# Stick-breaking attention heads: sums of later key blocks made by VectorE before the suffix products

## Chip, cores and metric
One core of one Trainium2 chip. The metric is device time in microseconds of one launch; lower is better.

## What is computed
A long fp32 program of two transformer-like blocks on 512 tokens of 1024 features. The part that matters here is the stick-breaking attention of the second block, 8 heads of 64 features:

```python
z = einsum('bqhd,bshd->bhqs', q, k) * scale
past = key_pos[None, :] < qpos[:, None]
log_keep = where(past, log_sigmoid(-z), 0.0)
suffix = cumsum(log_keep, axis=3, reverse=True) - log_keep   # sum over the later keys
w = where(past, exp(log_sigmoid(z) + suffix), 0.0)
out = einsum('bhqs,bshd->bqhd', w, v)
```

Beside it, on VectorE, the same stretch of time holds the top-k selection for the DSA attention that follows: for three blocks of 128 queries the 128 largest of 256, 384 and 512 scores, as a mask.

## The kernel before
Keys lie on the 128 partitions and queries along the free dimension. A head's scores are four key blocks `kt` = 0 to 3, of 512, 384, 256 and 128 queries (query blocks before the key block are causally empty). They stand behind one another at columns `ZOFF` = 0, 512, 1024, 896, + of a region of 1280 columns in PSUM; two regions take turns over the heads. Block 3 lies at 896 and block 2 at 1024, so each of them begins and ends inside a bank.

Each head h passes these steps:
- TensorE, `sb_scores(h)`: three fp32r products per key block (high and low halves) and the causal mask. From h = 2 on they wait for the exponential of head h - 2, whose region they overwrite, and for the low halves of their query and key jobs (`job_lo`).
- ScalarE, `sb_softplus(h)`: Abs, Exp and Ln over 1280 columns into `zw`.
- VectorE, `sb_max(h)` (L2578): max(z, 0) + zw into `spt`, which is the softplus, in fp32. It waits for the values of head h - 2, which read the same buffer of `spt`.
- TensorE, `sb_suffix(h)` (L1128): for each key block kt the sum of softplus over later keys is subtracted from z in PSUM: a product with `negtri` (-1 on the diagonal and on one side of it) for the block's own keys, and one with `negone` (all -1) for every later block k2. These are plain fp32 products, two recorded passes each. Loop: kt over 0 to 3, k2 over kt to 3.
- ScalarE: the exponential of the region into `spt` (L1784), the weights.
- TensorE, `sb_values(h)` (L1139): 10 products of 64 columns. VectorE, `sb_out(h)`: the copy of the head to `T0`.

Engines run their own lists in order, tied by semaphores. TensorE's list per head: `sb_suffix(h)`, transposes of a query job (`sb_job`, in heads 1 and 3; `dsa_job` in head 5), `sb_values(h - 1)`, `sb_scores(h + 2)`, transposes of a key job, which wait for the low half of the job before. VectorE's list per head (L2598 to L2620): `sb_max(h + 1)`, the low half of a job (heads 1, 3, 5), `sb_out(h - 1)`, column sums of loaded weights (`sum_step`), top-k steps (`topk`, max8 and match-replace, L2407 and L2409) as dealt out by `TOPK_SB`, in heads 1, 3 and 5 a second low half between them. After the last head all three masks `Mk` must be written (L2422) before TensorE goes on with `dsa_scores(1)` (L1205).

Of the kernel before, what the change touches and what calls it, by code (L numbers as in the profile page):

```python
# [6 lines left out]
ALU = mybir.AluOpType  # L7
# [7 lines left out]
P = 128  # L15
SEQ, CTX, D = 512, 256, 1024
# [50 lines left out]
ZOFF = (0, 512, 1024, 896)  # L67
# [82 lines left out]
def program(nc, t, out):  # L150
    ctx = ExitStack()
    with ctx:
# [3 lines left out]
        def sem(name):  # L156
            return ctx.enter_context(nc.semaphore(name))
# [47 lines left out]
        def s2(name, shape, dt=F32):  # L205
            return e2.enter_context(nc.sbuf_tensor(name, shape, dt))
# [12 lines left out]
        negtri = s2("negtri", [P, P])  # L219
        negone = s2("negone", [P, P])  # L220
# [5 lines left out]
                                                                     ("ixH", "ixL", "izH", "izL")])[1:]  # L226
        zw = s2("zw", [P, 2, 1280])
        spt = s2("spt", [P, 2, 1280])
        e2.close()


# [7 lines left out]
        def s3(name, shape, dt=F32):  # L239
# [80 lines left out]
        rp_rd, odd_rp, zero_rd, ixT, ix_hi, ix_lo, ixs_rd, ixr_rd, ix_acc, msk_rd = [sem(n) for n in (  # L320
            "rp_rd", "odd_rp", "zero_rd", "ixT", "ix_hi", "ix_lo", "ixs_rd", "ixr_rd", "ix_acc", "msk_rd")]
        jobT, job_hi, job_lo = sem("jobT"), sem("job_hi"), sem("job_lo")
        z_rd, zmin_rd, zexp_rd, zln_rd, sp_rd, arg_rd, wgt_rd, sv_rd, so_rd = [sem(n) for n in (
            "z_rd", "zmin_rd", "zexp_rd", "zln_rd", "sp_rd", "arg_rd", "wgt_rd", "sv_rd", "so_rd")]
        ds_rd, dmx_rd, dp_rd, dt_rd, dpv_rd, do_rd = [sem(n) for n in ("ds_rd", "dmx_rd", "dp_rd", "dt_rd", "dpv_rd", "do_rd")]
# [396 lines left out]
        def _(pe):  # L722
            mm, tr = nc.tensor.matmul, nc.tensor.transpose
# [7 lines left out]
            for j in range(4):  # L731
                last = tr(X[:, 0, VCW + TAPS * j:VCW + TAPS * j + TAPS], cwr[0:TAPS, j * P:j * P + P],
                          ident[0:TAPS, 0:TAPS])
# [241 lines left out]
            for j in range(4):  # L975
                last = mm(acc[:, 0, :], onesD[:], cy[:, j], start=(j == 0), stop=(j == 3))
# [3 lines left out]
            for j in range(4):  # L980
                for tt in range(TT):
                    last = tr(oTp[j][:, tt * P:tt * P + P], qtok[:, tt, j * P:j * P + P], ident[:])
                last.then_inc(oT, 1)
            for j in range(4):
                pe.wait_ge(csq_rd, j + 1)
                last = mm(acc[:, 3, :], onesD[:], sgt[:, j % 2], start=(j == 0), stop=(j == 3))
# [121 lines left out]
            def region(h):  # L1108
                return ps[:, 4 - 4 * (h % 2):7 - 4 * (h % 2), :].rearrange("p b n -> p (b n)")
# [18 lines left out]
            def sb_suffix(h):  # L1128
                z, s_ = region(h), spt[:, h % 2]
                pe.wait_ge(sp_rd, h + 1)  # L1130
                for kt in range(4):
                    for k2 in range(kt, 4):
                        w = SEQ - k2 * P
                        o0 = ZOFF[kt] + (k2 - kt) * P
                        last = mm(z[:, o0:o0 + w], negtri[:] if k2 == kt else negone[:], s_[:, ZOFF[k2]:ZOFF[k2] + w],
                                  start=False, stop=True, skip_group_check=True)
                last.then_inc(arg_rd, 1)

            def sb_values(h):  # L1139
# [36 lines left out]
            for h in range(NH):  # L1176
                sb_suffix(h)
                if h in (1, 3):
                    sb_job(h + 3)
                if h == 5:  # L1180
                    dsa_job(8)
                if h >= 1:
                    sb_values(h - 1)
                if h + 2 < NH:
                    sb_scores(h + 2)
                if h in SB_TURN:
                    pe.wait_ge(job_lo, h + 4)
                    turn_group(SB_TURN[h])
                if h in (1, 3):
                    sb_job(h + 4)  # L1190
                if h == 5:
                    dsa_job(9)
# [848 lines left out]
        def _(dve):  # L2041
            V = nc.vector
# [200 lines left out]
            q = tapped  # L2243
# [331 lines left out]
            def region(h):  # L2575
                return ps[:, 4 - 4 * (h % 2):7 - 4 * (h % 2), :].rearrange("p b n -> p (b n)")[:, 0:1280]

            def sb_max(h):  # L2578
                dve.wait_ge(zln_rd, h + 1)
                if h >= 2:  # L2580
                    dve.wait_ge(sv_rd, h - 1)
                V.scalar_tensor_tensor(spt[:, h % 2], region(h), 0.0, zw[:, h % 2], ALU.max, ALU.add).then_inc(sp_rd, 1)

            def sb_out(h):
                dve.wait_ge(sv_rd, h + 1)
                V.tensor_copy(T0[:, :, h * HD:h * HD + HD], ps[:, 3, 0:256].rearrange("p (t d) -> p t d", t=4))\
                    .then_inc(so_rd, 1)
# [3 lines left out]
            even_tile_out(4, 1)  # L2591
            topks(4, 1)
            sb_max(0)
            even_tile_out(4, 3)
            sb_low(2)
            sb_low(3)
            split_low(NC1 + 11)
            for h in range(NH):  # L2598
                steps = range(TOPK_SB[h], TOPK_SB[h + 1])
                if h + 1 < NH:  # L2600
                    sb_max(h + 1)
                if h in (1, 3):
                    sb_low(h + 3)
                if h == 5:
                    job_low(8, 0, 7, True)
                if h >= 1:
                    sb_out(h - 1)
                for kt in range(4):
                    if h < 4 and kt % 2 == 0:
                        sum_step(13, 2 * h + kt // 2)  # L2610
                    if kt == 1 and h in SB_TURN:
                        group_columns(SB_TURN[h])
                    if kt < len(steps) - 1:
                        topk(steps[kt])
                if h in (1, 3):
                    sb_low(h + 4)
                if h == 5:
                    job_low(9, 0, 7, False)
                if h < 7:
                    topk(steps[-1])  # L2620
# [428 lines left out]
```

## Time and profile before

| | us |
|---|---|
| median of 3 runs | 1762.8 |
| lowest, highest | 1760.67, 1763.5 |
| the profiled execution | 1767.19 |
| its span | 1765.5 |
| stage of the 8 heads (suffix of head 0 to the copy of head 7) | 489 to 577 |

The profile is one execution. Its page gives shares of the whole span; the order of time gives instructions of an engine with start, duration and, in brackets, the idle time before one and what ended it.

### The profile page before, as it was taken

How to read it: one execution, taken by the hardware profiler on the slowest of the kernel's cores; microseconds unless marked ns; L12 is line 12 of the kernel's file. 1: busy time of each engine (PE TensorE's matmuls, PEld its weight loads, DVE VectorE, ACT ScalarE, POOL GpSimd, SP SyncE). 2: the span in 40 equal slices, each digit the busy share in tenths (PEclk: the TensorE clock that was granted, in tenths of full speed). 3: DMA queues.
4: the chain of work that ended last, by engine and by line, in shares of the span. 5: the costliest groups of instructions: out<-in, count | busy, mean ns of one | idle time of the engine just before them, and what ended most of it. 6: DMA issues, size and time to landing. Idle time of an engine off the chain costs nothing.

```text
span 1765.5 us, 22789 instructions
## 1 busy us (share of the span) xinstructions
PE 1662.8 (94%) x8951; PEld 1370.4 (78%) x8957; DVE 1009.1 (57%) x1435; ACT 658.6 (37%) x887; POOL 322.9 (18%) x250
## 2 busy tenths in 40 slices
PE   4999999999898998999999999899979899999999
PEld 3897787888776886788887887777757688888887
DVE  3568898777878658533333345757576733333243
ACT  4323465432354424423332223434463533333121
POOL 0000000000000003788885011224301100000011
PEclk8999999999999999999999999999989999999999
DMA  7645300352210323565564323221102133332321
GB/s 270 216 144 190 97 1 1 116 177 85 95 52 21 96 93 100 165 184 179 184 189 161 113 86 95 73 72 48 49 25 72 51 116 95 95 95 89 130 88 48
DMA packets 145605, 187.93 MB, mean 106 GB/s; under 512 B 7053, under 2 KB 104565, under 8 KB 145524
## 3 DMA queue, kind: packets, MB, share of 16 engines
q1 hardware_dynamic: 145524, 186.82, 32.9%
q8 instruction: 55, 0.90, 0.2%
q14 instruction: 26, 0.21, 0.0%
HBM read 184.70 MB, written 2.10 MB: 106 GB/s over the span
## 4 chain that ended last, share of the span: by engine, by line
PE 64%; DVE 13%; POOL 9%; issue 6%; DMA 4%; ACT 3%; SPq 1%; another core or an unknown queue 0%; POOLq 0%; DVEq 0%; ACTq 0%
PE ps L841 7%; PE ps L843 7%; PE ps L842 7%; POOL mraw L628 4%; POOL msum L635 4%; DMA mraw<-in_w_mod_dram 3%; PE ps L1349 2%; PE ps L1351 2%; PE ps L1350 2%; PE ps L1346 2%; PE ps L1342 2%; PE ps L1343 2%; PE ps L1405 2%; PE ps L1407 2%; PE ps L1406 2%
## 5 line engine op out<-in xcount | busy, mean ns | idle before, releaser
L1537 ACT ACTIVATE whi<-wraw 128x2048 fp32r<-128x2048 f32 x71 | 135.8, 1913 | 305.0 <-PE ps L843 210.2
L2052 DVE TENSOR_TENSOR wlo<-wraw,whi 128x2048 fp32r<-128x2048 f32 x64 | 148.2, 2316 | 152.9 <-ACT whi L1537 152.7
L2808 DVE TENSOR_TENSOR wlo<-wraw,whi 128x2048 fp32r<-128x2048 f32 x22 | 51.5, 2341 | 203.4 <-ACT whi L1901 203.4
L1342 PE MATMUL ps<-uH,whi 128*128 128x512 f32 x352 | 141.2, 401 | 9.8 <-ACT uH L1869 8.3
L1343 PE MATMUL ps<-uH,wlo 128*128 128x512 f32 x352 | 139.7, 397 | 0.0
L841 PE MATMUL ps<-hH,whi 128*128 128x512 f32 x352 | 139.1, 395 | 0.0
L843 PE MATMUL ps<-hH,wlo 128*128 128x512 f32 x352 | 137.8, 391 | 0.0
L842 PE MATMUL ps<-hL,whi 128*128 128x512 f32 x352 | 137.7, 391 | 0.0
L1350 PE MATMUL ps<-uL,whi 128*128 128x512 f32 x352 | 136.9, 389 | 0.0
L1349 PE MATMUL ps<-uH,whi 128*128 128x512 f32 x352 | 136.9, 389 | 0.0
L1351 PE MATMUL ps<-uH,wlo 128*128 128x512 f32 x352 | 136.9, 389 | 0.0
L1346 PE MATMUL ps<-uL,whi 128*128 128x512 f32 x352 | 111.5, 399 | 4.2 <-DVE uL L2747 4.2
L635 POOL TENSOR_TENSOR msum<-msum,mraw 128x512 f32<-128x512 f32 x66 | 107.6, 1631 | 5.2
L841 PE MATMUL ps<-uH,whi 128*128 128x512 f32 x256 | 103.0, 402 | 0.0
L843 PE MATMUL ps<-uH,wlo 128*128 128x512 f32 x256 | 100.3, 392 | 0.0
L842 PE MATMUL ps<-uL,whi 128*128 128x512 f32 x256 | 100.2, 391 | 0.0
L628 POOL TENSOR_TENSOR mraw<-mraw,cpad 128x1024 f32<-128x1024 f32 x44 | 84.3, 1916 | 55.9 <-PE ps L756 43.1
L1905 ACT ACTIVATE whi<-wraw 128x2048 fp32r<-128x2048 f32 x22 | 42.2, 1919 | 137.3 <-PE ps L1351 137.3
L1898 ACT ACT_TABLE_LOAD x22 | 28.2, 1283 | 173.4 <-PE ps L1346 173.4
L2119 DVE SCALAR_TENSOR_TENSOR cy<-utp,cols,cy 128x512 f32<-128x512 f32 x116 | 87.0, 750 | 3.4
L1342 PEld LDWEIGHTS ps<-uH,whi 128*128 128x128 f32 x352 | 67.8, 193 | 26.2 <-issue 12.2
L1346 PEld LDWEIGHTS ps<-uL,whi 128*128 128x128 f32 x352 | 67.6, 193 | 19.7 <-DVE uL L2747 5.4
(500 smaller groups left out, 3839.7 us busy)
## 6 DMA issues: line engine op xcount, KB each, us to landing
mraw<-in_w_mod_dram SPq DMA_DIRECT2D x104, 512.0 KB, 3.8
wraw<-in_w_gate_dram SPq DMA_DIRECT2D x22, 1024.0 KB, 5.3
wraw<-in_w_up_dram SPq DMA_DIRECT2D x22, 1024.0 KB, 5.4
wraw<-in_w_down_dram SPq DMA_DIRECT2D x16, 1024.0 KB, 5.2
wraw<-in_w_in_dram SPq DMA_DIRECT2D x11, 1024.0 KB, 5.5
mfirst<-in_w_mod_dram SPq DMA_DIRECT2D x16, 512.0 KB, 7.6
wraw<-in_w_in_even_dram SPq DMA_DIRECT2D x8, 1024.0 KB, 6.3
wraw<-in_w_in_odd_dram SPq DMA_DIRECT2D x16, 512.0 KB, 4.5
```

Of the source, the lines that this page charges most:

```text
L628: g.tensor_tensor(w, w, cpad[:, 2 * kp:2 * kp + 2, 2:3].to_broadcast([P, 2, GW]), ALU.mult).then_inc(msum_rd, 1)
L635: g.tensor_tensor(msum[:], msum[:], w[:, kk], ALU.add).then_inc(msum_rd, 1)
L841: mm(o, h, xh[:, k0 + k], start=(first and k == 0), stop=False)
L842: mm(o, h, xl[:, k0 + k], start=False, stop=False)
L843: last = mm(o, l, xh[:, k0 + k], start=False, stop=(done and k == nk - 1))
L1342: mm(o[m], w_[0][m][:, k], uH[:, k], start=(k == 0), stop=False)
L1343: mm(o[m], w_[1][m][:, k], uH[:, k], start=False, stop=False)
L1346: last = mm(o[m], w_[0][m][:, k], uL[:, k], start=False, stop=(k == KT - 1))
L1349: mm(o[m], w_[0][m][:, k], uH[:, k], start=(k == 0), stop=False)
L1350: mm(o[m], w_[0][m][:, k], uL[:, k], start=False, stop=False)
L1351: last = mm(o[m], w_[1][m][:, k], uH[:, k], start=False, stop=(k == KT - 1))
L2052: V.tensor_tensor(wlo[:, n % 2, :], wraw[:, n % 2, :], whi[:, n % 2, :].bitcast(F32), ALU.subtract).then_inc(lo_done, 1)
```

## The change
For each head VectorE forms three sums of softplus blocks in a new buffer `later` (two heads, three blocks of 128 columns). In the kernel's layout they are: for queries of block 2, keys of blocks 1 + 2; for queries of block 3, blocks 2 + 3; and for queries of block 3, blocks 1 + 2 + 3. One `tensor_tensor` of 256 elements makes the first and second at once, one of 128 elements adds block 1 to the latter. Each is waited for by a semaphore of its own, `add_rd`.

TensorE first does the four triangular products of 512, 384, 256 and 128 columns, then three products of 128 columns with `negone` for the nearest later block, read straight from `spt`. Then it waits for the sums and does two products, of 128 and 256 columns. With `negone` this is 768 columns a head in five products, where it was 1280 in six. Nothing else moves.

```diff
+        later = s2("later", [P, 2, 3, P])
@@ sb_suffix(h), TensorE
                 for kt in range(4):
-                    for k2 in range(kt, 4):
-                        w = SEQ - k2 * P
-                        o0 = ZOFF[kt] + (k2 - kt) * P
-                        last = mm(z[:, o0:o0 + w], negtri[:] if k2 == kt else negone[:], s_[:, ZOFF[k2]:ZOFF[k2] + w],
-                                  start=False, stop=True, skip_group_check=True)
+                    r = slice(ZOFF[kt], ZOFF[kt] + SEQ - kt * P)
+                    mm(z[:, r], negtri[:], s_[:, r], start=False, stop=False, skip_group_check=True)
+
+                def later_keys(kt, q, blocks, x):
+                    o0 = ZOFF[kt] + (q - kt) * P
+                    return mm(z[:, o0:o0 + blocks * P], negone[:], x, start=False, stop=True, skip_group_check=True)
+
+                later_keys(2, 3, 1, s_[:, ZOFF[3]:ZOFF[3] + P])
+                later_keys(1, 2, 1, s_[:, ZOFF[2]:ZOFF[2] + P])
+                later_keys(0, 1, 1, s_[:, ZOFF[1]:ZOFF[1] + P])
+                pe.wait_ge(add_rd, 2 * h + 2)
+                later_keys(1, 3, 1, later[:, h % 2, 2])
+                last = later_keys(0, 2, 2, later[:, h % 2, 0:2, :].rearrange("p b n -> p (b n)"))
                 last.then_inc(arg_rd, 1)
@@ sb_max(h), VectorE
                 V.scalar_tensor_tensor(spt[:, h % 2], region(h), 0.0, zw[:, h % 2], ALU.max, ALU.add).then_inc(sp_rd, 1)
+                dve.wait_ge(sp_rd, h + 1)
+                if h >= 2:
+                    dve.wait_ge(arg_rd, h - 1)
+                s_, sums = spt[:, h % 2], later[:, h % 2]
+                others = s_[:, ZOFF[1] + P:ZOFF[1] + 5 * P].rearrange("p (i n) -> p i n", n=2 * P)[:, :, 0:P]
+                V.tensor_tensor(sums[:, 0:3:2], s_[:, ZOFF[2]:ZOFF[2] + 2 * P].rearrange("p (i n) -> p i n", n=P), others,
+                                ALU.add).then_inc(add_rd, 1)
+                dve.wait_ge(add_rd, 2 * h + 1)
+                V.tensor_tensor(sums[:, 1], sums[:, 2], s_[:, ZOFF[1] + 2 * P:ZOFF[1] + 3 * P], ALU.add).then_inc(add_rd, 1)
```

## Rows read from the trace of the kernel before

**Rows 1.** The page: span, then engine, busy us, share, instructions
```profile
span 1765.5 us, 22789 instructions
...
PE 1662.8 (94%) x8951; PEld 1370.4 (78%) x8957; DVE 1009.1 (57%) x1435; ACT 658.6 (37%) x887; POOL 322.9 (18%) x250
```

**Rows 2.** The chain that ended last, 538 to 600: start us, us, what
```profile
549.23 1.49 DVE spt L2582
...
570.66 0.44 DVE Mk L2422
...
571.14 0.58 PE ps L1205
```

**Rows 3.** TensorE in order of time: start, us, line, operands, [idle before <-releaser]
```profile
497.35 0.47 PE L1122 MATMUL ps<-uH 128*128 128x512 f32 x1 [3.52 <-ACT spt L1784]
...
511.30 1.02 PE L1135 MATMUL ps<-spt,negtri 128*128 128x512 f32 x2
...
512.16 1.46 PE L1135 MATMUL ps<-spt,negone 128*128 128x384 f32 x6
...
515.64 2.34 PE L1146 MATMUL ps<-T,spt 128*128 128x64 f32 x20
...
531.10 0.66 PE L1105 MATMUL ps<-ident,T 128*128 128x128 f32 x4 [1.23 <-DVE uL L2569]
...
538.60 0.50 PE L1122 MATMUL ps<-uH 128*128 128x512 f32 x1 [0.34 <-DVE uL L2566]
...
560.93 1.12 PE L1135 MATMUL ps<-spt,negtri 128*128 128x512 f32 x2 [1.68 <-DVE spt L2582]
...
571.14 0.58 PE L1205 MATMUL ps<-uH 128*128 128x256 f32 x1 [3.02 <-DVE Mk L2422]
```

**Rows 4.** VectorE in order of time, the same columns
```profile
508.66 1.49 DVE L2582 SCALAR_TENSOR_TENSOR spt<-ps,zw 128x1280 f32<-128x1280 f32 x1 [4.19 <-PE ps L1146]
...
511.00 0.74 DVE L2323 SCALAR_TENSOR_TENSOR msum<-mraw,cpad,msum 128x512 f32<-128x512 f32 x1
...
511.66 0.55 DVE L2407 MAX8 m<-work 128x8 f32<-128x384 f32 x1
...
518.73 1.49 DVE L2582 SCALAR_TENSOR_TENSOR spt<-ps,zw 128x1280 f32<-128x1280 f32 x1
...
528.95 1.49 DVE L2582 SCALAR_TENSOR_TENSOR spt<-ps,zw 128x1280 f32<-128x1280 f32 x1
...
540.10 1.49 DVE L2582 SCALAR_TENSOR_TENSOR spt<-ps,zw 128x1280 f32<-128x1280 f32 x1
...
549.23 1.49 DVE L2582 SCALAR_TENSOR_TENSOR spt<-ps,zw 128x1280 f32<-128x1280 f32 x1 [2.82 <-PE ps L1146]
...
559.38 1.49 DVE L2582 SCALAR_TENSOR_TENSOR spt<-ps,zw 128x1280 f32<-128x1280 f32 x1 [0.24 <-PE ps L1146]
...
569.15 0.75 DVE L2420 SCALAR_TENSOR_TENSOR ptd<-ptd,cnt 128x512 f32<-128x512 f32 x1
...
569.93 0.69 DVE L2421 TENSOR_TENSOR work<-work,ptd 128x512 f32<-128x512 f32 x1
```

**Rows 5.** VectorE by shape: line, operation, shape, count | busy us, mean ns
```profile
L2481 DVE TENSOR_TENSOR tmp<-T,ropet 128x256 f32<-128x256 f32 x4 | 1.7, 417 | 0.0
...
L2160 DVE TENSOR_TENSOR tmp<-kvt,ropet 128x128 f32<-128x128 f32 x2 | 0.6, 284 | 0.0
...
L2894 DVE TENSOR_TENSOR tmp<-T,ropet 128x256 f32<-128x256 f32 x6 | 4.7, 775 | 0.0
```

**Rows 6.** Stretches of 2 us: busy by engine (count), then PEclk, DMA share, GB/s
```profile
498.00:500.00 2.00, 2.00 (x12) 1.54 (x11) 1.97 (x3) 0.00 (x0) 0.00 (x0) 0.67 0.00 0
...
502.00:504.00 2.00, 2.00 (x9) 1.28 (x8) 1.93 (x6) 1.94 (x3) 0.00 (x0) 0.98 0.00 0
...
570.00:572.00 2.00, 0.86 (x4) 0.77 (x5) 1.58 (x4) 0.35 (x2) 0.00 (x0) 0.59 0.00 0
...
580.00:582.00 2.00, 1.86 (x16) 1.62 (x15) 1.10 (x2) 0.80 (x4) 0.00 (x0) 0.85 0.00 0
```

More of the change, by code:

```diff
@@ L322, in program @@
         jobT, job_hi, job_lo = sem("jobT"), sem("job_hi"), sem("job_lo")
+        add_rd = sem("add_rd")
         z_rd, zmin_rd, zexp_rd, zln_rd, sp_rd, arg_rd, wgt_rd, sv_rd, so_rd = [sem(n) for n in (
```

## Prediction

> **What bounds the kernel now.** I read the page first [rows 1]: TensorE is busy for 94% of the span, VectorE for 57%. That average would make a cut of TensorE work look like a gain and added VectorE work look free. So I looked only at the stage that is changed, from 485 to 577 us. The chain that ended last [rows 2] passes from TensorE to `sb_max(6)` at 549.23 and closes the stage on VectorE: the mask `Mk` of the top-k selection is written at 570.66, and only then does TensorE go on at 571.14 with the DSA scores, after 3.02 us without work.
>
> TensorE's order of time [rows 3] shows one head: suffix products at 511.30, and the values of the head before at 515.64. After that it waits for VectorE four times in the stage: 1.23 us at 531.10 (for the low halves of job 6), 0.34 us at 538.60 (for those of job 7), 1.68 us at 560.93 (for `sb_max(7)`) and 3.02 us at 571.14. VectorE's order of time [rows 4] is the other side: it waits 4.19 us at 508.66, then runs from `sb_max(2)` without a wait through `sb_max(3)` (518.73), `sb_max(4)` (528.95) and `sb_max(5)` (540.10), waits 2.82 us at 549.23 and 0.24 us at 559.38, both for the values on TensorE, and is not idle again before the mask. Between its 8 maxima it works through the top-k steps that `TOPK_SB` dealt out. So the two engines are nearly even, VectorE ends the stage, and TensorE has time left.
>
> **TensorE's saving.** The products of a head with the full matrix go from 1280 columns to 768, those with the triangle stay at 1280. The 512 columns saved are as many as the first triangular product has: its two passes start at 511.30 and the next product at 512.16 [rows 3], so 0.86 us a head, off a suffix of 4.34 us (511.30 to 515.64); 3.48 us are left. For eight heads that is 6.9 us of TensorE work.
>
> **VectorE's addition.** Two adds a head. The 256-element add takes 0.417 us in the mean of four in the rotation of the DSA queries and the 128-element one 0.284 us [rows 5]; one of the same 256-element shape takes 0.775 us in a later stage where GpSimd works too. GpSimd has nothing to do in this stage after 489 us, so I take the lower one and keep the other as an end. The adds wait for results of VectorE itself. A waited instruction starts 0.03 us after its predecessor's end (569.15 + 0.75 to 569.93), an unwaited one 0.08 us before it (511.00 + 0.74 to 511.66) [rows 4]. So a head pays 0.11 us because the first add must see `sb_max` finished, 0.42 + 0.03 us for the first add, 0.28 - 0.08 us for the second: A = 0.77 us, 6.1 us for eight heads. Ends: 0.54 us (the two durations less an overlap of 0.08 each, as if no wait cost anything) and 1.13 us (the slow row in place of 0.42).
> The Trainium skill ("VectorE: DVE Perf Modes", The DRAIN you can't avoid) says of a semaphore between two operations that it "costs nothing extra here". The two spacings above do not agree: 0.11 us. By that rule A would be at its lower end and the sum below 1.15 us smaller; the rows decide.
>
> **New waits.** TensorE waits for the second add only after four triangular products and three single blocks, 1280 + 384 columns, 0.86 x 1664/512 = 2.8 us after it could start; the adds are ready 0.75 us after the maximum. This wait is free. Its cover would be gone only if the adds took over 2.8 us. VectorE's new wait for the suffix of two heads before (`arg_rd`) is met before the maximum can start, as that waits for later work. Behind the adds on VectorE stand the low halves, the copy of the finished head, the column sums (with them the issue of the next weight loads on the SyncE queue) and the top-k steps: all are 0.77 us late for each add before them. That is the real price.
>
> **The sum, head by head**, as shifts against the old times (+ is later):
> - Heads 0 and 1 before `sb_max(2)`: the first saving is lost, since scores(2) wait at 497.35 for ScalarE's exponential [rows 3], which was behind its own work. The adds of heads 0 and 1 go into VectorE's 4.19 us of idle time. Suffix(1) ends 0.86 earlier, so `sb_max(2)` starts at -0.86.
> - `sb_max(3)`: VectorE ran without a wait, -0.86 + 0.77 = -0.09. `sb_max(4)`: +0.68. Low half of job 7 (L2566, which ends the wait at 538.60 [rows 3]): behind the adds of head 4, +1.45. `sb_max(5)` the same.
> - TensorE: scores(6) wait for that low half, so +1.45; suffix(5) gives back 0.86; values(4), for which `sb_max(6)` waits, are at +0.59. VectorE alone would be at 1.45 + 0.77 - 2.82 = -0.60, so TensorE sets it: `sb_max(6)` at +0.59. VectorE's big idle of 2.82 us shrinks to 1.2 and does not vanish.
> - `sb_max(7)`: 0.59 + 0.77 - 0.24 = +1.12. The mask: 1.12 + 0.77 = +1.89.
> In one line: 5A - 2 x 0.86 - 0.24 = +1.89 us. Five adds lie on the path, two savings do, the other six savings lie beside waits. TensorE's last gap grows to about 5.3 us.
> After 571 us nothing in the chain is tied to a fixed time. Later waits (TensorE waits once for GpSimd's sums near 957 us) shift as a whole, so I pass the delay on fully. With A = 0.54 the sum is +0.74, with A = 1.13 +3.7.
>
> **The clock.** The granted clock [rows 6] is 0.67 from 498 to 500 and 0.98 from 502 to 504: TensorE ran at the lower level (1.2 GHz) from about 498.7 to 502.1, after the 3.52 us wait. Likewise from about 570.4 (0.59 of full over 570 to 572) to 580.6 (0.85 over 580 to 582), around the 3.02 us wait; that stretch ended in sparse work. The waits of 1.23 and 1.68 us brought no fall. In the new kernel the wait before job 7's transposes grows from 1.23 us: scores(5) end 0.9 earlier, the low half of job 6 comes 0.68 + 0.77 later, 3.6 us in all. If the clock falls there for a stretch like the first (3.4 us), TensorE loses 1.7 us; 1.2 us of that lies under its wait for job 7's low half (0.34 us before; the low half is 1.45 us later and suffix(4) with values(3) only 0.59: 1.2 us), leaving 0.5 us. I add these 0.5 us: +2.4 us. The longer waits at 493 and 568 may move the other two stretches by a microsecond or two: +-0.9 us, no sign taken.
>
> The profiled execution took 1767.2 us (span 1765.5), 0.25% over the median 1762.8 of the runs; the sum is made against the profile and +2.4 us carried to the median: **1765.2 us**.
>
> **Rivals.**
> 1. *The clock falls and stays* (slower). Place: suffix(4) and values(3), after the new 3.6 us gap. Point: from 2.4 us at the lower level on, all that is lost (half of each microsecond) is no longer covered. With a stretch as long as the second one (10.2 us) TensorE loses 5.1, 1.2 of it covered: +3.9 on top of 1.9, 1768.6 us. For it: both waits over 3 us are tied to the lower level. Against: the suffix is dense work, and after 497.35 dense work had the higher level back in 4.7 us. The Trainium skill ("TensorE: Matmul & The Clock Gate", HAM oscillation — how this bites in real kernels) describes just this, a gap for input after which TensorE restarts at half rate, and speaks against any change that widens such gaps. Beside it, the slow 256-element add (A = 1.13) gives +3.7 + 0.5, 1767.0 us. Together 25%.
> 2. *The adds are as good as hidden* (no change). A at its lower end, and the stretch at 571 us no longer than its work: 1762 to 1763.5 us. For it: VectorE idles 7.3 us in the stage. Against: 4.2 of these lie before the part that matters. 14%.
> 3. *TensorE is the bound* (faster). Where the page's 94% held for this stage too, eight savings would count, less what ScalarE covers in head 0: 7 x 0.86 = 6.0, 1756.8 us. Against: TensorE's four waits for VectorE. A partial form, where VectorE catches up through its wait at 549.23, still needs the adds at under half their rows to pass -3.5 us. 6%.
> The forecast itself, +0.8 to +3.5 us, has 55%.
>
> **How the numbers follow.** 0.2% is 3.5 us, about what a measurement here can tell from no change (the three runs span 2.8 us). Faster by more: 0.06. Within: the forecast, rival 2 and the weaker part of rival 1: 0.70. Slower by more: 0.24. Range: below, rival 2 with a run's spread, 1761.5; above, the long low-clock stretch, 1769.0.
>
> **What would show it.** Right: a suffix of 3.5 us a head with no wait inside; adds of 0.42 and 0.28 us right behind each maximum; VectorE without a wait from `sb_max(2)` to the end of head 4; an idle of 1 to 2 us before `sb_max(6)`; a 3 to 4 us wait of TensorE before job 7's transposes; `Mk` near 572.5 and TensorE idle for 5 us before it. Wrong: a wait at the second group of products, an add of 0.7 us, a mask earlier than 570, or a later stage that absorbs the shift or doubles it.

## The result and the profile after

| | before | after |
|---|---|---|
| median, us | 1762.8 | 1767.58 |
| lowest, highest of 13 runs each | 1758.8, 1764.67 | 1763.99, 1774.97 |
| ratio, 95% interval | | 1.0034 (1.0021 to 1.0046) |
| the profiled execution (its span) | 1767.19 (1765.5) | 1770.69 (1769.0) |

The change costs time: by the ratio 6.0 us of 1762.8, between 3.7 and 8.1, by the medians 4.8. The two profiled executions lie 3.5 us apart. Forecast were +2.4 us, in a range up to 1769.0, and, at 70%, "not to be told from no change"; the slower side, by more than 3.5 us, had 24%, and the interval of the ratio lies on that side. All ratios are of fast executions alone: they leave out one of topk_behind_filled, of 9255.55 us, and two of the kernel before, of 2368.17 and 3299.25 us.

The page of after, span and engines:

```profile
span 1769.0 us, 22785 instructions
...
PE 1658.8 (94%) x8941; PEld 1366.5 (77%) x8941; DVE 1014.6 (57%) x1451; ACT 658.7 (37%) x887; POOL 323.7 (18%) x250
```

TensorE works 4.0 us less than in [rows 1] and VectorE 5.5 us more, and the shares are the same 94% and 57%. The page gives no hint of why the kernel is slower.

TensorE in order of time, the same columns as in [rows 3]; suffix(2) begins at 511.23:

```profile
496.44 0.77 PE L1124 MATMUL ps<-uH 128*128 128x512 f32 x1 [4.37 <-ACT spt L1794]
...
500.85 2.88 PE L1135 MATMUL ps<-spt,negtri 128*128 128x512 f32 x8
...
511.23 2.32 PE L1135 MATMUL ps<-spt,negtri 128*128 128x512 f32 x8
513.39 0.83 PE L1139 MATMUL ps<-spt,negone 128*128 128x128 f32 x6
514.06 0.82 PE L1139 MATMUL ps<-later,negone 128*128 128x128 f32 x4
514.72 2.34 PE L1156 MATMUL ps<-T,spt 128*128 128x64 f32 x20
```

Four triangular products in a row (x8: two passes each), three with `negone` on softplus blocks, two on the sums. From 511.23 to 514.72 it takes 3.49 us, where it took 4.34, and between its groups no wait is shown. Its waits later in the stage:

```profile
532.60 1.12 PE L1107 MATMUL ps<-ident,T 128*128 128x128 f32 x4 [3.66 <-DVE uL L2579]
...
562.39 3.78 PE L1135 MATMUL ps<-spt,negtri 128*128 128x512 f32 x8 [2.32 <-DVE spt L2592]
...
573.39 0.48 PE L1215 MATMUL ps<-uH 128*128 128x256 f32 x1 [2.99 <-DVE Mk L2432]
...
574.33 4.37 PE L1156 MATMUL ps<-T,spt 128*128 128x64 f32 x20
```

The wait before job 7's transposes has grown from 1.23 to 3.66 us, the one before suffix(7) from 1.68 to 2.32; before the DSA scores it is 2.99 us, as it was (3.02), only 2.25 us later, and not the 5 us I had expected, as the suffix of head 7 ran at the lower clock (below) and took 5.25 us (562.39 to 567.64) in place of 3.49. The last line is the values of head 7, which ran at the lower clock before the change too:

```profile
572.18 4.37 PE L1146 MATMUL ps<-T,spt 128*128 128x64 f32 x20
```

VectorE in order of time:

```profile
497.39 1.49 DVE L2592 SCALAR_TENSOR_TENSOR spt<-ps,zw 128x1280 f32<-128x1280 f32 x1
...
507.81 1.49 DVE L2592 SCALAR_TENSOR_TENSOR spt<-ps,zw 128x1280 f32<-128x1280 f32 x1 [3.46 <-PE ps L1156]
509.33 0.42 DVE L2598 TENSOR_TENSOR later<-spt 128x256 f32<-128x256 f32 x1
509.79 0.29 DVE L2601 TENSOR_TENSOR later<-later,spt 128x128 f32<-128x128 f32 x1
...
518.67 1.49 DVE L2592 SCALAR_TENSOR_TENSOR spt<-ps,zw 128x1280 f32<-128x1280 f32 x1
...
529.67 1.49 DVE L2592 SCALAR_TENSOR_TENSOR spt<-ps,zw 128x1280 f32<-128x1280 f32 x1
...
541.60 1.49 DVE L2592 SCALAR_TENSOR_TENSOR spt<-ps,zw 128x1280 f32<-128x1280 f32 x1
```

```profile
550.12 1.49 DVE L2592 SCALAR_TENSOR_TENSOR spt<-ps,zw 128x1280 f32<-128x1280 f32 x1 [1.42 <-PE ps L1156]
...
560.85 1.49 DVE L2592 SCALAR_TENSOR_TENSOR spt<-ps,zw 128x1280 f32<-128x1280 f32 x1
...
572.91 0.43 DVE L2432 TENSOR_SCALAR Mk<-work 128x512 bf16<-128x512 f32 x1
```

Each maximum is followed by its two adds, 0.42 and 0.29 us. There is no wait shown from 507.81 to the end of head 4; before `sb_max(6)` it is 1.42 us where it was 2.82 in [rows 4]. The clock of TensorE in stretches of 2 us, columns as in [rows 6]:

```profile
494.00:496.00 2.00, 0.00 (x0) 0.00 (x0) 1.46 (x2) 1.98 (x2) 0.00 (x0) 0.76 0.00 0
496.00:498.00 2.00, 1.55 (x5) 0.97 (x5) 1.97 (x2) 0.30 (x1) 0.00 (x0) 0.50 0.00 0
...
500.00:502.00 2.00, 2.00 (x8) 1.48 (x8) 1.90 (x7) 0.91 (x1) 0.00 (x0) 0.54 0.02 4
...
532.00:534.00 2.00, 1.40 (x5) 1.25 (x6) 2.00 (x4) 1.01 (x2) 0.00 (x0) 0.64 0.00 0
534.00:536.00 2.00, 2.00 (x4) 0.81 (x3) 1.90 (x6) 1.00 (x2) 0.00 (x0) 0.50 0.00 0
...
564.00:566.00 2.00, 2.00 (x7) 1.48 (x6) 1.90 (x6) 0.00 (x0) 0.00 (x0) 0.50 0.00 0
```

I measure the stage from the start of `sb_max(1)` to the start of the last mask `Mk`, both on VectorE. Before: 498.30 to 570.66, 72.36 us. After: 497.39 to 572.91, 75.52 us, so **+3.16 us**. Two lines of the kernel before on which this and a later reading rest are `sb_max(1)` on VectorE and the start of suffix(1) on TensorE:

```profile
498.30 1.49 DVE L2582 SCALAR_TENSOR_TENSOR spt<-ps,zw 128x1280 f32<-128x1280 f32 x1
```

```profile
500.64 1.79 PE L1135 MATMUL ps<-spt,negtri 128*128 128x512 f32 x2
```

The stretch ahead of the stage was 0.91 us shorter in this execution, though nothing is changed there, and the one behind it 1.3 us longer (1769.0 - 572.91 = 1196.1 against 1194.8).

How long TensorE was at the lower clock in the whole execution can be added up from windows of 4 us: about 99 us in both profiled executions. The changed one had 10 us more of it between 480 and 588 (25 against 15), and 7 us less from there to the end (51 against 58). So more time at the lower clock does not explain the 1.3 us behind the stage; they stay open.

### The profile page after: what moved, and what is told of

The parts are those of the page before. It is cut to its first block, busy times and chain, and to the rows that moved or that the text cites. A ratio compares the mean times of both kernels' runs of the same rounds, so it can differ in the third digit from the quotient of the medians.

```text
span 1769.0 us, 22785 instructions
## 1 busy us (share of the span) xinstructions
PE 1658.8 (94%) x8941; PEld 1366.5 (77%) x8941; DVE 1014.6 (57%) x1451; ACT 658.7 (37%) x887; POOL 323.7 (18%) x250
## 4 chain that ended last, share of the span: by engine, by line
PE 63%; DVE 14%; POOL 9%; issue 6%; DMA 4%; ACT 4%; SPq 1%; POOLq 0%; DVEq 0%; ACTq 0%
PE ps L843 7%; PE ps L844 7%; PE ps L845 7%; POOL mraw L630 4%; POOL msum L637 4%; DMA mraw<-in_w_mod_dram 2%; PE ps L1352 2%; PE ps L1360 2%; PE ps L1353 2%; PE ps L1356 2%; PE ps L1359 2%; PE ps L1361 2%; PE ps L1415 2%; PE ps L1417 2%; PE ps L1416 2%
```

## Experiments

All were timed in 5 rounds against the kernel before on the same chip. "Stage" is the interval defined above, from each kernel's profiled execution; "to `dsa_scores(1)`" is from the same start to the DSA scores on TensorE that need the last mask; "rest" is from the last mask to the end of the span.

| kernel | ratio (95%) | stage, us | to `dsa_scores(1)`, us | rest, us |
|---|---|---|---|---|
| before | 1 | 72.36 | 72.84 | 1194.8 |
| after | 1.0034 (1.0021 to 1.0046) | 75.52 | 76.00 | 1196.1 |
| triangles_first | 0.9995 (0.9984 to 1.0005) | 72.30 | 72.78 | 1191.2 |
| adds_alone | 1.0039 (1.0024 to 1.0053) | 79.49 | 79.97 | 1195.1 |
| saving_alone | 0.9997 (0.9986 to 1.0009) | 71.14 | 71.62 | 1196.3 |
| adds_twice | 1.0043 (1.0029 to 1.0057) | 78.69 | 79.17 | 1194.4 |
| adds_behind | 1.0011 (0.9998 to 1.0024) | 74.57 | 75.05 | 1192.9 |
| before_filled | 0.9969 (0.9956 to 0.9982) | 70.91 | 72.12 | 1190.0 |
| after_filled | 0.9991 (0.9977 to 1.0005) | 77.85 | 78.33 | 1190.0 |
| before_topk_early | 0.9966 (0.9951 to 0.9982) | 67.50 | 69.48 | 1191.8 |
| after_topk_early | 0.9950 (0.9931 to 0.9968) | 66.99 | 68.61 | 1190.7 |
| before_topk_filled | 0.9948 (0.9933 to 0.9964) | 66.10 | 69.41 | 1191.6 |
| topk_adds_behind | 0.9953 (0.9937 to 0.9968) | 65.03 | 65.51 | 1191.6 |
| topk_behind_filled | 0.9961 (0.9943 to 0.9978) | 64.49 | 64.97 | 1191.7 |

The theory (VECTOR): VectorE ends the stage; five pairs of adds lie on its path to the mask and two savings of TensorE count. The rival (CLOCK): the adds are as good as hidden, and the loss comes from wider waits of TensorE and the lower clock behind them.

**The order alone** (triangles_first).

```diff
 for kt in range(4):
-    for k2 in range(kt, 4): ... negtri if k2 == kt else negone ...
+    negtri product of the block
+for kt in range(3):
+    for k2 in range(kt + 1, 4): ... negone ...   # all 1280 columns
```

> The order alone: all four triangular products, then the six with the full matrix, 1280 columns each, no sums. All theories: no change, within 0.5 us; each suffix 4.34 us as before. If alternating the stationary matrices cost TensorE anything, it would be faster by that, up to 8 x 0.2 = 1.6 us.

Ratio 0.9995, stage 72.30 for 72.36 us. The order is neutral, and no gain from fewer changes of the stationary matrix can be seen.

**The adds alone** (adds_alone): the changed VectorE, the old products on TensorE. Before its last block TensorE waits for the sums, which are ready long before.

```diff
 for kt in range(4):
+    if kt == 3:
+        pe.wait_ge(add_rd, 2 * h + 2)
     for k2 in range(kt, 4): ... as before, 1280 columns with negone ...
```

> VectorE makes the sums as in the changed kernel, TensorE keeps its 1280 columns with the full matrix and does not read the sums. Theory VECTOR (VectorE's adds of heads 2 to 7 lie on the path to the masks, 0.77 us each, the first in idle time): the mask 5 x 0.77 = 3.9 us later against the stage's start, total +3.9 to +5 us. Theory CLOCK (the adds are as good as hidden, the loss comes from wider waits of TensorE and the lower clock after them): the waits widen less than in the changed kernel as nothing ends earlier on TensorE, total 0 to +1 us.

Ratio 1.0039, which is 6.9 us (4.2 to 9.3; VECTOR expected 3.9 to 5, CLOCK 0 to 1), and the stage is 7.1 us longer, 3.3 us more than VECTOR's 3.85. Neither theory alone gives that. Two starts of `sb_max` on VectorE (heads 4 and 5), then the clock at 532 and at 538:

```profile
530.12 1.49 DVE L2586 SCALAR_TENSOR_TENSOR spt<-ps,zw 128x1280 f32<-128x1280 f32 x1
...
543.24 1.49 DVE L2586 SCALAR_TENSOR_TENSOR spt<-ps,zw 128x1280 f32<-128x1280 f32 x1 [1.23 <-PE ps L1150]
```

```profile
532.00:534.00 2.00, 0.95 (x5) 0.96 (x6) 1.97 (x6) 1.97 (x2) 0.00 (x0) 0.52 0.00 0
...
538.00:540.00 2.00, 2.00 (x10) 1.51 (x9) 1.92 (x5) 0.00 (x0) 0.00 (x0) 0.77 0.50 126
```

From `sb_max(4)` to `sb_max(5)` it takes 13.12 us, where it took 11.15 us. One add pair explains 0.78 of the 1.97. The rest goes with the lower clock around a wait of 2.83 us: it is down for 6.8 us (0.52 at 532 to 534, 0.77 at 538 to 540), and `sb_max(5)`, which never waited before, now waits 1.23 us for TensorE's values. Here my first rival (the clock falls and stays) happens in a shorter form (6.8 us, not 10.2), in a kernel other than the one it was made for. The interval before it, `sb_max(1)` to (2), has 0.85 us more than before, with the clock down for 6.8 us and the adds in idle time; the one behind, to `sb_max(6)`, 1.13 us more, as TensorE now leads. The other four, (2) to (4) and (6) to the mask, are each longer by 0.79 to 0.80 us: the price A, on the path.

**The saving alone** (saving_alone): the sums are left out, and TensorE reads single softplus blocks in their place.

```diff
-pe.wait_ge(add_rd, 2 * h + 2)
-later_keys(1, 3, 1, later[:, h % 2, 2])
+later_keys(1, 3, 1, s_[:, ZOFF[2] + P:ZOFF[2] + 2 * P])
```

> TensorE streams 768 columns with the full matrix as in the changed kernel, but reads blocks of the softplus itself in place of the sums, and VectorE makes no sums; the sums over later keys are left out so. Theory VECTOR: two of eight savings count and 0.24 us of idle time, mask 2.0 us earlier, 1.1 us if the clock falls before scores(2); total -1 to -2 us. Rival TENSOR (TensorE is the bound): 7 x 0.86 = -6 us. Theory CLOCK: 0 to +2 us, since TensorE's waits get wider as in the changed kernel.

```profile
547.11 1.49 DVE L2591 SCALAR_TENSOR_TENSOR spt<-ps,zw 128x1280 f32<-128x1280 f32 x1 [1.97 <-PE ps L1155]
...
557.05 1.49 DVE L2591 SCALAR_TENSOR_TENSOR spt<-ps,zw 128x1280 f32<-128x1280 f32 x1
...
568.34 0.43 DVE L2431 TENSOR_SCALAR Mk<-work 128x512 bf16<-128x512 f32 x1
```

Stage -1.22 us, total unchanged (0.9997). VECTOR had -2.0, or -1.1 with the clock down before scores(2), and it was down there (6.8 us from 494.4). `sb_max(6)` still waits 1.97 us, and behind it VectorE does not wait until the mask at 568.34. So 6.9 us less of TensorE's work are worth 1.2 us; that TensorE is the bound is out. CLOCK's +0 to +2 does not fit the stage; the total (-2.5 to +1.6 us) cannot tell it from VECTOR's -1 to -2.

**The adds twice** (adds_twice).

```diff
 second add .then_inc(add_rd, 1)
+dve.wait_ge(add_rd, 4 * h + 2)
+the same two adds again
```

> The changed kernel with its two adds made twice, one after another. Theory VECTOR: 5 x 0.77 = 3.9 us more than the changed kernel, the mask +5.7 us against the kernel before and +7 with the clock's part; total about +9 to +10 us. Theory CLOCK: the same as the changed kernel, +5 to +6 us, as long as the second pair is ready before TensorE asks for it (1.5 us after the maximum, TensorE asks after 2.8 us).

Ratio 1.0043, stage +6.33 us against before and +3.17 against after (VECTOR: +5.7 and +3.9; CLOCK: nothing against after). The stage decides for VECTOR. The total does not: it is 7.6 us over the kernel before, where VECTOR had 9 to 10 and CLOCK 5 to 6, and 1.0043 and 1.0034 overlap. The first step of the chain is of interest, heads 1 and 2 on VectorE and the clock there:

```profile
496.72 1.49 DVE L2592 SCALAR_TENSOR_TENSOR spt<-ps,zw 128x1280 f32<-128x1280 f32 x1
...
506.17 1.49 DVE L2592 SCALAR_TENSOR_TENSOR spt<-ps,zw 128x1280 f32<-128x1280 f32 x1 [1.71 <-PE ps L1156]
```

```profile
496.00:498.00 2.00, 2.00 (x7) 1.25 (x6) 1.97 (x2) 0.00 (x0) 0.00 (x0) 0.52 0.03 8
498.00:500.00 2.00, 2.00 (x11) 1.75 (x11) 1.86 (x6) 0.09 (x1) 0.00 (x0) 0.63 0.00 0
```

Here 9.45 us pass from `sb_max(1)` to `sb_max(2)`; in the kernel before it was 10.36, so -0.91 us, and I had forecast -0.86 for the changed kernel. In the changed kernel it was 10.42. The difference is the clock: here it is down for 3.4 us as in the kernel before (0.52 and 0.63), there for 6.8 us (0.76 at 494 to 496, 0.54 at 500 to 502). The wait was 3.40 us here and 4.37 us there. The second pair of adds costs 0.8 us in five of the six later steps, as the first pair does, and 0.2 before `sb_max(6)`: of the 3.17 us over the changed kernel, these are 4.1, and the first step gives 1.0 back.

**The adds behind the low halves** (adds_behind).

```diff
 sb_max(h + 1)                      # without the adds
 low half of job 4, 6 or 8 (heads 1, 3, 5)
+sb_sums(h + 1)                     # the two adds
```

> The changed kernel with the adds of heads 2, 4 and 6 behind the low halves of jobs 4, 6 and 8 on VectorE, where they stood ahead of them. The sums are ready 1.5 to 2.2 us after the maximum, TensorE asks after 2.8 us. Theory VECTOR: VectorE's list is as long as before, so the mask stays where it is (75.5 us after the start of sb_max(1)), within 0.5 us; only TensorE's waits for low halves shrink by 0.77 us (the one before job 7 from 3.7 to 2.9 us, where the clock may then stay up). Total as the changed kernel, +5 to +6 us, or +4 to +5 without that stretch. Rival LOW HALVES (the adds cost because low halves stand behind them): 3 x 0.77 = 2.3 us under the changed kernel.

```profile
527.28 1.49 DVE L2592 SCALAR_TENSOR_TENSOR spt<-ps,zw 128x1280 f32<-128x1280 f32 x1
528.68 0.68 DVE L2579 SCALAR_TENSOR_TENSOR uL<-ps,uH 128x512 fp32r<-128x512 f32 x1
529.28 0.42 DVE L2600 TENSOR_TENSOR later<-spt 128x256 f32<-128x256 f32 x1
529.73 0.29 DVE L2603 TENSOR_TENSOR later<-later,spt 128x128 f32<-128x128 f32 x1
```

Stage 74.57 us, 0.95 less than after, where VECTOR allowed 0.5 and the rival wanted 2.3. A part VECTOR had not thought of is in these lines: the low half starts 1.40 us after the maximum and the add 0.60 us after the low half, so neither pays the 0.11 us of waiting for its predecessor. Three heads save 0.12 us each, 0.37 us lie before `sb_max(2)`, and 0.24 us before `sb_max(6)`. TensorE's wait before job 7 is 2.88 us and the clock still fell. The total is 1.0011, the interval reaching from 0.9998 to 1.0024: 4 us under the changed kernel by the ratios, more than the stage explains. It is also less than the 4 to 6 us over the kernel before that VECTOR had expected. Where the other 3 us are is not settled; the two ratios are each against other runs of the kernel before, and each has 2 us to either side. Part of it may be the clock, whose mean over the runs is 0.9749 here and 0.9732 in the changed kernel.

**The waits filled** (before_filled, after_filled): products whose results nobody reads, in TensorE's idle time.

```diff
 def sb_scores(h):
+    if h == 2:
+        fill(7, 5)        # 4 in before_filled; each 128 x 512, fp32, 0.86 us
 sb_values(2):
+    fill(3, 3)            # after_filled alone
 dsa_scores(0)
+fill(6, 3)
```

> The kernel before with the same fill where it waits: four before scores(2), three between dsa_scores(0) and (1). VECTOR + CLOCK: 1.7 us come back at 499 to 502 and some 4 us at 571 to 581, total -4 to -6 us. So the gap between the kernels, both filled, is what VectorE's adds alone cost: +4 to +5 us here... worked out as 5 x 0.77 - 2 x 0.86 - 0.24 = +1.9 us if only the path counts, +4 if more than half of the stretches were in both. VECTOR alone: 0.

> The changed kernel with extra products in TensorE's idle time, whose results nobody reads: five of 512 fp32 columns (0.86 us each) before scores(2), three before values(2) (they move the 3.7 us wait before job 7 ahead, where VectorE does not need values(2) yet), three between dsa_scores(0) and (1). Theory VECTOR + CLOCK: the granted clock stays at its upper level over the four stretches; what the lower level cost TensorE on the path comes back: 0.9 us at 495 to 502, 0.5 us at 533 to 536, and some 4 us at 573 to 584 (values(7) 4.4 us for 2.3 among it). The mask comes 1.4 us earlier, total 5 to 6 us under the changed kernel, so 0 to -1 us against the kernel before. Theory VECTOR alone (the clock has no part in it): total as the changed kernel, +5 to +6 us, the mask unchanged.

TensorE in before_filled, the fill (L1113) and then values(7):

```profile
569.39 2.79 PE L1113 MATMUL ps<-xT,ident 128*128 128x512 f32 x6
...
572.49 2.34 PE L1152 MATMUL ps<-T,spt 128*128 128x64 f32 x20
```

values(7) takes 2.34 us, for 4.37 in the kernel before and in the changed one (574.33 above). The rest of the program is 4.8 us shorter (1190.0 for 1194.8), the stage 1.45 us, the ratio 0.9969, which is 5.5 us: as expected. At the next head's first DSA products (L1208 at 581.92 before, L1214 at 578.87 here), behind both stretches, the filled kernel is 4.3 us ahead, counted from `sb_max(1)`; the interval of the ratio is 3.2 to 7.8 us. So the lower clock behind these two waits costs the old kernel 4 us or more. A third thing changed by itself: suffix(7), which came behind a wait of 1.68 us in both kernels, now ran at the lower clock for 3.4 us, where before it did not. The stage does not show that, since VectorE's mask comes later anyway:

```profile
562.00:564.00 2.00, 2.00 (x5) 1.21 (x5) 1.90 (x5) 0.00 (x0) 0.00 (x0) 0.50 0.01 4
```

In after_filled the rest is 1190.0 us too, but the stage got longer, 77.85 us, where I had expected the mask 1.4 us earlier. The fill before values(2) kept the clock up at 528, and it fell 8.5 us later:

```profile
534.00:536.00 2.00, 0.82 (x8) 0.68 (x7) 1.92 (x4) 0.00 (x0) 0.00 (x0) 1.00 0.75 245
536.00:538.00 2.00, 2.00 (x9) 1.37 (x10) 1.93 (x4) 0.00 (x0) 0.00 (x0) 0.72 0.05 17
```

TensorE had waited 1.18 us (0.82 busy of 534 to 536) behind values(3), and the clock is at the lower level from 536.9 for 10.2 us, over scores(6) and suffix(5). VectorE then waits for TensorE, so that `sb_max(6)` comes 13.2 us after `sb_max(5)`, where the changed kernel needs 8.5. The ratio is 0.9991, 1.6 us under before and 7.6 under the changed kernel by the ratios; 5 to 6 were expected. The total bears the clock's part out (its runs have a mean granted clock of 0.9782, those of the changed kernel 0.9732); the profiled stage shows that one of the falls was not removed by the fill, but came at another place and cost more there.

**VectorE relieved** (before_topk_early, after_topk_early): seven of 25 top-k steps move ahead of head 0's loop, into VectorE's waits, and the rest is dealt out anew.

```diff
-TOPK_SB = (23, 26, 30, 33, 37, 40, 44, 48, 48)
+TOPK_SB = (30, 32, 35, 38, 41, 44, 46, 48, 48)
-(4, 1): range(21, 23)
+(4, 1): range(21, 26)
 sb_low(2)
+for r_ in range(26, 30): topk(r_)
 sb_low(3)
```

> The kernel before with top-k steps dealt out earlier: three more steps before sb_max(0), where VectorE waits 5.5 us, four between the low halves of jobs 2 and 3 (5.9 us), two in head 0 (4.2 us), so 18 steps instead of 25 in the heads. Theory VECTOR: the stage becomes TensorE's; suffix(4) 1.2 us, suffix(6) 1.8 us earlier, the mask near 566 in place of 570.7 and TensorE's 3 us wait before it gone, with it the lower clock after it: total -5 to -9 us. If VectorE's order were not the bound: 0.

> The changed kernel with the same earlier top-k steps. Theory VECTOR: now TensorE's saving counts, 0.86 us in each of heads 2, 4, 6 and 7, and about nothing in 1, 3 and 5, where a low half stands behind the adds (0.77): 3.7 us under the kernel before with the same move, total -8 to -12 us. Theory that the adds or their waits cost TensorE something by themselves: not faster than the kernel before with the same move.

The kernel before with this edit, VectorE's last maximum and the mask, then TensorE at the point where it used to wait 3 us:

```profile
555.65 1.49 DVE L2582 SCALAR_TENSOR_TENSOR spt<-ps,zw 128x1280 f32<-128x1280 f32 x1 [1.37 <-PE ps L1146]
...
563.90 0.43 DVE L2422 TENSOR_SCALAR Mk<-work 128x512 bf16<-128x512 f32 x1
```

```profile
563.32 2.34 PE L1146 MATMUL ps<-T,spt 128*128 128x64 f32 x20
...
565.88 0.37 PE L1205 MATMUL ps<-uH 128*128 128x256 f32 x1
```

The mask is written before TensorE needs it, `dsa_scores(1)` follows `dsa_scores(0)` at once, and the stage is 4.86 us shorter (4.8 expected). Ratio 0.9966, 6.0 us. VECTOR's first half is shown: the end of the stage was VectorE's. In such a stage the change is no longer a loss: 0.9950 beside 0.9966. The intervals overlap, and the stage is only 0.51 us shorter where the expectation had 3.7.

In this kernel and the next ones TensorE waits for the mask not at all or for some 0.1 us, so my stage ends at the wrong event; the column "to `dsa_scores(1)`" is the one to read. By it these top-k steps are worth 3.36 us (72.84 to 69.48), and the change on top of them 0.87 us (68.61). In after_topk_early the clock was down twice for 6.8 us in the stage, in its partner twice for 3.4.

**Both remedies** (topk_adds_behind, topk_behind_filled, before_topk_filled): the edits above combined; the fills are five, or four, products before scores(2).

> The changed kernel with the earlier top-k steps and the adds behind the low halves. In this stage TensorE's waits of 0.70, 1.05 and 1.42 us for low halves are on the path. VECTOR: up to 0.77 us off each, 2.2 us in all under the kernel with the earlier top-k steps alone; total -10 to -12 us.

> The same with five products of 512 fp32 columns, unread, in TensorE's wait of 4.4 us before scores(2). CLOCK: the lower level from 494 to 501 us does not come; TensorE gains 2.3 us there, of which 1.2 us count (VectorE's idle time before sb_max(2)). Total 1.2 us under the one without the fill, -11 to -13 us. Without a part of the clock: the same as without the fill.

> The kernel before with the earlier top-k steps and four such products before scores(2). CLOCK: 1.2 to 1.7 us under the kernel before with the earlier top-k steps, total -7 to -8 us. It is the partner of the one above: the difference of the two is what the sums on VectorE are worth in a stage in which VectorE has room: savings of TensorE in heads 2, 4, 6 and 7 and parts of 1, 3 and 5, 3.5 to 5 us.

To the mask they take 65.03, 64.49 and 66.10 us, to `dsa_scores(1)` 65.51, 64.97 and 69.41. By the latter the adds behind the low halves are worth 3.10 us here (68.61 to 65.51; up to 2.2 expected), with 3.4 us at the lower clock in place of 6.8 at both places, and the five fills 0.54 (1.2 expected). With everything, the change is worth 4.44 us, 64.97 against 69.41, where 3.5 to 5 were expected; by the mask it would look like 1.6. About 1.3 of the 4.44 are the clock: from suffix(7) to `dsa_scores(0)` it takes 9.60 us in before_topk_filled, with 6.8 us at the lower level, and 7.43 in topk_behind_filled, with 3.4, and only 0.86 of that difference is the saving. That leaves some 3.1 us for the change. These are TensorE's two lines, of before_topk_filled and of topk_behind_filled:

```profile
566.67 0.37 PE L1211 MATMUL ps<-uH 128*128 128x256 f32 x1
```

```profile
558.84 0.39 PE L1221 MATMUL ps<-uH 128*128 128x256 f32 x1
```

VectorE in topk_behind_filled, `sb_max(7)` and the mask:

```profile
549.32 1.49 DVE L2598 SCALAR_TENSOR_TENSOR spt<-ps,zw 128x1280 f32<-128x1280 f32 x1 [0.54 <-PE ps L1162]
...
558.36 0.43 DVE L2438 TENSOR_SCALAR Mk<-work 128x512 bf16<-128x512 f32 x1
```

From `sb_max(7)` to the mask it takes 9.04 us; in before_topk_filled 8.25 (555.11 to 563.36). There the add pair is on VectorE's path to the mask again, though TensorE hardly waits for that mask now, as from `sb_max(2)` to (3) and (4) to (5), 10.3 us each and 0.1 longer than in the partner, where VectorE had waited 0.47 and 0.46 us for ScalarE inside those steps. From (5) to (6) and (6) to (7), where TensorE is the bound, it is 1.3 and 0.9 us shorter. In total time nothing of it can be seen: 0.9961 and 0.9948, intervals overlapping, and it stays open where the 4.4 us go. As totals, topk_adds_behind has -8.3 us (-10 to -12 expected), topk_behind_filled -6.9 (-11 to -13) and before_topk_filled -9.2 (-7 to -8). All five kernels with the earlier top-k steps beat both kernels of this case, and before_topk_filled, without the change, has the lowest ratio by a margin that is within its interval.

## Why the prediction was right or wrong

By its own steps:

1. *VectorE ends the stage.* Shown, by saving_alone (TensorE's 6.9 us worth 1.2), by adds_twice (+3.2 us of stage) and by before_topk_early (the mask 4.9 us earlier, TensorE's next work 3.4). One reading was wrong: TensorE waited for VectorE five times in the stage and not four. The wait left out is 0.61 us at 552.08, before the transposes of head 5, for the low half of job 8; it is 1.42 us after the change (at 553.75). No term of the sum used it, and the step from `sb_max(6)` to (7) came out right.
2. *The saving, 0.86 us a head.* 4.34 - 3.49 = 0.85. *The adds, A = 0.77.* From `sb_max(3)` to the copy of head 1 it took 1.41 us before and 2.19 after (518.67 to 520.86): 0.78. The 0.11 us for waiting on its own result are there too: the first add starts 1.52 us after its maximum, a low half 1.40. The Trainium skill ("VectorE: DVE Perf Modes", The DRAIN you can't avoid) has a semaphore between two operations "costs nothing extra here"; these rows do not agree, and by it the sum would have come out 1.15 us lower.
3. *The new wait of TensorE is free.* No idle time is shown before the products on the sums.
4. *The shifts.* Against the start of `sb_max(1)`, in us:

| | `sb_max(2)` | (3) | (4) | (5) | (6) | (7) | mask |
|---|---|---|---|---|---|---|---|
| said | -0.86 | -0.09 | +0.68 | +1.45 | +0.59 | +1.12 | +1.89 |
| measured | +0.06 | +0.85 | +1.63 | +2.41 | +1.80 | +2.38 | +3.16 |

Behind the first column, each step from one to the next holds within 0.25 us, so which savings and adds count was told rightly. What fails is the first column, by 0.92 us, and it runs through to the end. Suffix(1) did save; but the lower clock, which came 1.3 us into scores(2) before, was there when they started (0.50 of full over 496 to 498), and they took 4.41 us (496.44 to 500.85) for 3.29. The prediction had this stretch down as "+-0.9 us, no sign taken". This is the mis-sized term: put at nothing, it measured +0.92 us. That the longer wait (3.52 to 4.37 us, by TensorE's own saving) brought the longer stretch is likely but not shown: topk_adds_behind had a wait of 4.17 us and the short stretch, adds_alone one of 3.52 and the long one. In adds_twice, with 3.40 us, the same step measured -0.91.
5. *The clock before job 7*, +0.5: the wait was 3.66 us for 3.6 said, the clock fell for 3.4 us, and `sb_max(6)` lost 0.25 us more than the chain alone gives. Right in place, half in size. The Trainium skill ("TensorE: Matmul & The Clock Gate", HAM oscillation — how this bites in real kernels) tells of a restart at half rate behind a gap; the trace agrees in this place (0.50 from 534 to 536). When the clock falls these traces do not tell: in after_filled it fell behind a wait of 1.18 us, and [rows 3] shows 1.68 us without a fall. A fall that the prediction did not have came before suffix(7), behind a wait of 2.32 us. It cost nothing at the mask, and its 1.8 us are most of what TensorE's wait before the DSA scores is short of the 5.3 us that I expected (2.99).
6. *"I pass the delay on fully."* The profile has +2.25 us at the mask and +3.5 at the end. 1.3 us are added behind the stage, with less time at the lower clock there than before. This was no step of the sum. In the profiles of the seven kernels whose clock fell at the DSA scores, the rest holds the same instructions and varies from 1191.2 to 1196.3 us, so one execution can't tell 1.3 us from chance.

So of the 6.0 us (3.7 to 8.1) measured, the stage accounts for 3.2 in the profiled execution: 1.9 by the two engines, 1.2 by the clock.

For the rest one more number helps, the mean granted clock that each run has. Within one kernel the time falls by about 1 us for each 0.001 of it (an estimate, fitted over 199 runs of all kernels; in the changed kernel from 1774.97 us at 0.968 to 1763.99 at 0.977). The 13 runs of the changed kernel have 0.9732 in the mean. Those of the kernel before beside the experiments have 0.9755 (72 of 74 runs; two stand at 0.953 with an ordinary time), and for its 13 runs beside the changed kernel no clock is on record. By this estimate 2.3 of the 6.0 us are the clock, over the whole program, and 3.7 are left (1.4 to 5.8), in which the 1.9 of the sum lie. The same estimate gives before_filled (0.9801) 4.5 of its 5.5 us. The profiled pair has 0.972 on both sides, so its +3.5 us hardly hold the clock's mean part. That the medians lie 4.8 us apart and inside the range is thus no proof of the sum: it had 1.9 us right, and the range took in what the clock added. The chance of 24% for "slower" was too small, as I had counted the effects of the clock as even, while the mean clock of the changed kernel is lower.

## What to carry to other kernels

Before work is moved from one engine to another, find which engine the end of that stage waits for; here the busy shares (94% and 57%) pointed the wrong way, and the list of waits the right one. An add pair of 0.77 us beat a saving of 0.86 us because five of the eight adds lay on the path and only two of the savings did. Where an engine's list is the bound, a new step is cheapest behind the instruction that others wait for, and the better edit is to move old work out of that list first: with seven top-k steps put into VectorE's waits the mask came 4.9 us earlier and TensorE's next work 3.4 us. And once the bound has moved to the other engine, the end of the stage must be read there: by the mask the change looked like 1.6 us in the last pair of kernels, by TensorE's next work it was 4.4, of which 1.3 were the clock.

## What the runs showed of the hardware

The cost of TensorE's lower clock was larger than I had taken it for. In before_filled some 6 us of unread products brought 5.5 us of total time, and values(7) went from 4.37 to 2.34 us. Idle time alone does not foretell a fall. The same wait of 1.68 us before suffix(7) passed without one in before and triangles_first, and in before_filled and all five kernels with the earlier top-k steps the clock was down around it for 3.4 us (four of them) or 6.8 us (two). The clock fell behind a wait of 1.18 us in after_filled, and stayed up through one of 1.19 us at the same place in saving_alone, each behind values(3). The wait before scores(2) was followed by 3.4 us at the lower level in five executions and by 6.8 us in five. Of the five with a wait of 3.4 to 3.5 us (before, triangles_first, adds_twice, before_topk_early, adds_alone) four had the short stretch and adds_alone the long one; of the five with 4.2 to 4.4 us (after, saving_alone, adds_behind, after_topk_early, topk_adds_behind) four had the long one and topk_adds_behind the short. Executions of nearly the same program differ by microseconds, and the mean granted clock goes with it: the profiled one of triangles_first is 8 us shorter than that of before, with a stage of the same length, and has 0.980 where that of before has 0.972.
